# Value products of two attention stages from whole fp32 operands, two halves of the output partitions at a time

## The reference

```
s = jnp.where(mask, s, -jnp.inf)
p = jax.nn.softmax(s, axis=-1).astype(v.dtype)
outs.append(jnp.einsum('bhqk,bkhd->bqhd', p, v[:, :kend]))
...
a = jnp.where(mask, jnp.exp(jax.nn.log_sigmoid(z) + suffix), 0.0)
return jnp.einsum('bhqk,bkhd->bhqd', a, vf)
```

## Time and profile before

| what | value |
|---|---|
| median of 3 runs | 2650.02 us (2649.67 to 2657.27) |
| the profiled execution | 2650.2 us |
| its span in the profile | 2648.4 us |
| granted TensorE clock, mean | 0.996 |
| PE busy | 2569.6 us, 97% |
| PEld / DVE / ACT / POOL busy | 78% / 62% / 40% / 43% |

### The profile page before, as it was taken

One profiled execution on the slowest core, in us unless ns is written; L12 is line 12 of the kernel. 1 busy time (PEld: TensorE's weight loads), 2 busy tenths in 40 slices (PEclk: granted clock), 3 DMA queues, 4 the chain that ended last, 5 costly groups with the idle time before them and its releaser, 6 DMA issues.

```text
span 2648.4 us, 32612 instructions
## 1 busy us (share of the span) xinstructions
PE 2569.6 (97%) x12496; PEld 2055.2 (78%) x12496; DVE 1651.3 (62%) x1992; ACT 1055.4 (40%) x1502; POOL 1146.2 (43%) x1422
## 2 busy tenths in 40 slices
PE   8999999999999999999999999989999999999998
PEld 7877878687787887877776777757888888888886
DVE  6636663768648658567777566674455565555556
ACT  3627881436305315225366656673201111111132
POOL 4633344532432432432432222224565567655653
PEclk9999999999999999999999999999999999999999
DMA  3111002222112212111220010102111111111312
GB/s 139 48 52 32 17 25 93 83 66 96 56 48 73 64 48 73 64 56 64 107 92 24 25 32 24 33 16 103 52 53 45 52 56 56 50 46 48 121 47 80
DMA packets 44820, 156.32 MB, mean 59 GB/s; under 512 B 4928, under 2 KB 5312, under 8 KB 44672
## 3 DMA queue, kind: packets, MB, share of 16 engines
q1 hardware_dynamic: 31392, 110.11, 12.7%
q10 hardware_dynamic: 13280, 44.17, 4.7%
HBM read 141.55 MB, written 12.71 MB: 58 GB/s over the span
## 4 chain that ended last, share of the span: by engine, by line
PE 83%; DVE 9%; ACT 5%; issue 3%; POOL 1%; ACTq 0%; DVEq 0%; POOLq 0%
PE PS L787 37%; PE PS L1461 13%; PE PS L1487 10%; PE PS L1117 4%; PE PS L1024 3%; PE PS L1509 2%; PE PS L1150 1%; PE PS L923 1%; PE PS L1160 1%; PE PS L1372 1%; PE PS L1154 1%; PE PS L937 1%; DVE sb_softplus L2965 1%; PE PS L1333 1%; ACT mla_p L1686 1%
## 5 line engine op out<-in xcount | busy, mean ns | idle before, releaser
L640 POOL CAST w_hi<-w_stage 128x1024 fp32r<-128x1024 f32 x130 | 145.5, 1120 | 1047.9 <-PE PS L787 757.0
L643 POOL TENSOR_TENSOR w_lo<-w_stage,w_hi 128x256 fp32r<-128x256 f32 x520 | 496.7, 987 | 10.4
L787 PE MATMUL PS<-XH,w_hi 128*128 128x512 f32 x1216 | 385.3, 398 | 7.5 <-ACT ssd_z L1901 3.3
L787 PE MATMUL PS<-XL,w_hi 128*128 128x512 f32 x1216 | 376.4, 391 | 0.0
L787 PE MATMUL PS<-XH,w_lo 128*128 128x512 f32 x1216 | 375.6, 390 | 0.0
L787 PEld LDWEIGHTS PS<-XH,w_hi 128*128 128x128 f32 x1216 | 222.9, 188 | 61.3 <-issue 9.7
L787 PEld LDWEIGHTS PS<-XL,w_hi 128*128 128x128 f32 x1216 | 228.8, 188 | 48.9
L787 PEld LDWEIGHTS PS<-XH,w_lo 128*128 128x128 f32 x1216 | 228.8, 188 | 48.8
L714 POOL TENSOR_TENSOR w_lo<-w_stage,w_hi 128x256 fp32r<-128x256 f32 x260 | 220.1, 854 | 0.0
L710 POOL CAST w_hi<-w_stage 128x256 fp32r<-128x256 f32 x260 | 126.3, 489 | 184.9 <-PE PS L1461 107.6
L1461 PE MATMUL PS<-raw_hi,w_hi 128*128 128x512 f32 x512 | 158.0, 390 | 0.0
(11 more groups left out here) (466 smaller groups left out, 5541.3 us busy)
## 6 DMA issues: line engine op xcount, KB each, us to landing
w_stage<-w SPq DMA_DIRECT2D x202, 512.0 KB, 3.3
ssd_sum_rows<-sums_kept ACTq DMA_DIRECT2D x32, 512.0 KB, 3.7
H<-x_t ACTq DMA_DIRECT2D x8, 512.0 KB, 8.1
pj_kept<-ple_proj_tiles ACTq DMA_DIRECT2D x8, 512.0 KB, 2.6
h_kept<-H ACTq DMA_DIRECT2D x8, 512.0 KB, 3.4
H<-h_kept ACTq DMA_DIRECT2D x4, 1024.0 KB, 5.5
out_t<-out_tiles SPq DMA_DIRECT2D x16, 256.0 KB, 2.1
x_again<-x_t ACTq DMA_DIRECT2D x12, 256.0 KB, 3.0
```

The source lines that it names most:

```text
L640: nc.gpsimd.tensor_copy(w_hi[:, slot, :, :], w_stage[:, slot, :, :]).then_inc(s_w_hi, 1)
L643: nc.gpsimd.tensor_tensor(w_lo[:, slot, k:k + 2, :], w_stage[:, slot, k:k + 2, :], w_hi[:, slot, k:k + 2, :].bitcast(F32), ALU.subtract).t ...
L787: mm = nc.tensor.matmul(outs[:, half, :], wt[:, slot, k, :], a[:, k - first, half * HB:(half + 1) * HB], start=(k == whole[0] and wt is w_ ...
```

## The change

In MLA the turned chunk is copied once, as fp32, by DVE (`chunk_copy`); ACT's `chunk_hi` is gone, `v_lo` too, and `VM` holds the values alone. `chunk_values` multiplies tile by tile: even key tiles into output partitions 0 to 63, odd ones into 64 to 127, 128 queries at a time, so that neighbouring products go to opposite halves. In the chunk of rows 0 and 1 the first tile is split by its partitions into two products of 64 rows. `low_part` and `add_low` stay: what they join is now the even and the odd key tiles. In SB the weights are multiplied as they are, where they stand (`ZS`); the key's scale `RK`, which was part of the copy, goes into the values (`v_scaled`, one DVE instruction in place of ACT's and DVE's two). The two heads of a pair go to the two halves of one bank, 128 queries at a time, and one DVE copy (`attended`) takes them out. ACT's weight copy, `low_parts` and `v_hi` and DVE's `weights_lo`, `add_parts` and `v_lo` are gone. Semaphores are renamed and their counts changed to match.

```diff
@@ PE, MLA
             def chunk_values(u, c):
...
-                pe.wait_ge(s_tlo, n + 1)
+                pe.wait_ge(s_tcp, n + 1)
                 b, q0 = 6 + i // 2, i % 2 * 2 * P
-                for src in (PTH, PTL):
+                late = int(p == i)
+                for q in range(2):
                     for e in range(2):
-                        late = P if e and p == i else 0
-                        mm = nc.tensor.matmul(PS[:, b, q0 + late:q0 + 2 * P], VM[:, u % 2, 2 * p + e, :],
-                                              src[:, n % 4, 2 * P * e:2 * P * (e + 1) - late],
-                                              start=(c in (0, 7) and e == 0 and src is PTH), stop=True, skip_group_check=True)
+                        o, cols_ = slice(64 * e, 64 * e + 64), slice(q0 + P * q, q0 + P * (q + 1))
+                        if q >= e * late and (i or q):
+                            at_ = 2 * P * e + P * (q - e * late)
+                            mm = nc.tensor.matmul(PS[o, b, cols_], VM[:, u % 2, 2 * p + e, :], PT[:, n % 4, at_:at_ + P],
+                                                  start=(c in (0, 7) and q == 0), stop=True, skip_group_check=True)
+                        elif i == 0:
+                            nc.tensor.matmul(PS[o, b, cols_], VM[o, u % 2, 0, :], PT[o, n % 4, 0:P], start=False, stop=True, skip_group_check=True)
@@ PE, SB
             def sb_values(m, t):
...
-                pe.wait_ge(s_wl, T + 1)
-                if first:
-                    pe.wait_ge(s_at, 4 * m + 2 * hf) if m or hf else None
-                for src, slot in ((WH, T % 2), (WL, T % 3)):
+                pe.wait_ge(s_w, T + 1)
+                if first and m:
+                    pe.wait_ge(s_at, 4 * m - 2 + 2 * hf)
+                for q in range(q0, HB, P):
                     for u in range(2):
-                        mm = nc.tensor.matmul(PS[:, 4 + u, q0:HB], VHL[:, j, u, :], src[:, slot, u, q0:HB],
-                                              start=(first and src is WH), stop=True, skip_group_check=True)
+                        o = slice(64 * u, 64 * u + 64)
+                        mm = nc.tensor.matmul(PS[o, 4 + hf, q:q + P], VS[:, j, o], ZS[:, T % 3, u, q:q + P],
+                                              start=(first and q == q0), stop=True, skip_group_check=True)
@@ ACT, MLA: chunk_hi and its ten calls per head go
-            def chunk_hi(u, c):
...
-                nc.scalar.activation(PTH[:, n % 4, 0:wide], PS[:, 4 + n % 2, 0:wide], ACT.Copy).then_inc(s_thi, 1)
@@ ACT, SB: v_hi and low_parts go, and in each step
-                    if 1 <= step <= NU:
-                        act.wait_ge(s_w, T1 + 1)
...
-                        nc.scalar.activation(WH[:, T1 % 2, :, q1:HB], a, ACT.Copy, scale=RK[:, j1:j1 + 1]).then_inc(s_wh, 1)
@@ DVE, MLA: v_lo goes
-            def chunk_lo(u, c):
+            def chunk_copy(u, c):
                 n, wide = NCH * u + c, chunk_width(c)
-                dve.wait_ge(s_thi, mla_high("chunk", u, c))
-                v.tensor_tensor(PTL[:, n % 4, 0:wide], PS[:, 4 + n % 2, 0:wide], PTH_f[:, n % 4, 0:wide], ALU.subtract).then_inc(s_tlo, 1)
+                dve.wait_ge(s_tp, n + 1)
+                if n >= 4:
+                    dve.wait_ge(s_pv, n - 3)
+                v.tensor_copy(PT[:, n % 4, 0:wide], PS[:, 4 + n % 2, 0:wide]).then_inc(s_tcp, 1)
@@ DVE, SB: v_lo, add_parts and weights_lo go
+            def v_scaled(m):
+                dve.wait_ge(s_vt, m + 1)
+                v.tensor_tensor(VS[:, :, :], PS[:, 2:4, :].rearrange("p b (t d) -> p (b t) d", d=P),
+                                RK[:, 0:KT].unsqueeze(2).to_broadcast([P, KT, P]), ALU.mult).then_inc(s_vl, 1)
+
+            def attended(m, hf):
+                dve.wait_ge(s_o, NU * m + (NU if hf else 4))
...
+                v.tensor_copy(ATT[:, m, hf * HB:(hf + 1) * HB], PS[:, 4 + hf, :]).then_inc(s_at, 2)
```

More of the change, by code:

```diff
@@ L160 @@
 NCH = len(MLA_CHUNKS)
[L161 to L166, removed]
 MLA_RING = [("q", 0), ("k", 0), ("v", 0)]
@@ L332, in program @@
         LOW, at = place(at + TOK * 4, "mla_low_part", [P, TOK], F32)
-        (QH, QL, KH, KL, VM, PB, PTH, PTL, TRIG, NMX, SUMS), _ = region([
+        (QH, QL, KH, KL, VM, PB, PT, _, TRIG, NMX, SUMS), _ = region([
             ("mla_q_hi", [P, 2, TOK], F32R), ("mla_q_lo", [P, 2, TOK], F32R), ("mla_k_hi", [P, 2, TOK], F32R),
-            ("mla_k_lo", [P, 2, TOK], F32R), ("mla_v_hi_lo", [P, 2, KT, P], F32R), ("mla_p", [P, 4, TOK], F32),
-            ("mla_p_hi", [P, 4, HB], F32R), ("mla_p_lo", [P, 4, HB], F32R), ("trig", [P, TOK], F32),
+            ("mla_k_lo", [P, 2, TOK], F32R), ("mla_v", [P, 2, KT, 64], F32), ("mla_p", [P, 4, TOK], F32),
+            ("mla_p_turned", [P, 4, HB], F32), ("mla_spare", [P, 3, TOK], F32), ("trig", [P, TOK], F32),
             ("mla_neg_max", [P, 2, 8], F32), ("mla_sums", [P, 2, 8], F32)])
@@ L345, in program @@
         QL_f, _ = place(base[0] + 2 * TOK * 4, "mla_q", [P, 2, TOK], F32)
-        QH_f, KH_f, PTH_f = (t[:, :, :].bitcast(F32) for t in (QH, KH, PTH))
+        QH_f, KH_f = (t[:, :, :].bitcast(F32) for t in (QH, KH))
         (XR, TN, SQN, MU, RS), _ = region([
@@ L390, in program @@
         SPH, at = place(at, "sb_softplus_hi", [P, 3, 2, HB], F32R)
-        WH, at = place(at, "sb_weight_hi", [P, 2, 2, HB], F32R)
+        _, at = place(at, "sb_spare", [P, 2, 2, HB], F32)
         QHI, at = place(at, "sb_q_hi", [P, TOK], F32R)
@@ L395, in program @@
         KLO, at = place(at, "sb_k_lo", [P, TOK], F32R)
-        VHL, at = place(at, "sb_v_hi_lo", [P, KT, 2, P], F32R)
+        VS, at = place(at, "sb_v", [P, KT, P], F32)
+        _, at = place(at, "sb_spare_v", [P, KT, P], F32)
         vt_at = at
@@ L399, in program @@
         CC, at = place(at, "conv_gated", [P, TOK], F32)
-        OS, at = place(at, "sb_out_low_part", [P, HB], F32)
+        _, at = place(at, "sb_spare_out", [P, HB], F32)
         REST_R, at = place(at, "rest_r", [P, P], F32R)
@@ L2156, in _ @@
                         head_square(3)
-                    if step in (5, NU + 1):
-                        low_parts(m, int(step > 5))
-                    if step == NU + 1 and m < 3:
-                        v_hi(m + 1)
                     for key in sb_finished(m, step, 1):
@@ L2880, in sb_tap @@
                         v.tensor_tensor(y, y, RM[:, :], ALU.mult).then_inc(mix["c"].sem, 1)
-            def v_lo(m):
-                dve.wait_ge(s_vh, m + 1)
-                v.tensor_tensor(VHL[:, :, :, 64:128].rearrange("p t u d -> p (t u) d"),
-                                PS[:, 2:4, :].rearrange("p b (x d) -> p (b x) d", d=64),
-                                VHL[:, :, :, 0:64].bitcast(F32).rearrange("p t u d -> p (t u) d"), ALU.subtract).then_inc(s_vl, 1)
-            def add_parts(m, hf):
-                dve.wait_ge(s_os, 4 * m + 2 * hf + 2)
+            def v_scaled(m):
[4 more added lines that the diff above has]
+                dve.wait_ge(s_o, NU * m + (NU if hf else 4))
                 if m == 0 and hf == 0:
                     dve.wait_ge(s_hk, 16 * KT)
-                for u in range(2):
-                    low = OS[64:128, :] if u == 0 else OS[0:64, :]
-                    v.tensor_tensor(ATT[64 * u:64 * u + 64, m, hf * HB:(hf + 1) * HB], PS[0:64, 4 + u, :], low, ALU.add).then_inc(s_at, 1)
-            def weights_lo(m, t):
-                q0, T = SB_WIDE[t], NU * m + t
-                dve.wait_ge(s_wh, T + 1)
-                j = SB_UNITS[t][1]
-                v.scalar_tensor_tensor(out=WL[:, T % 3, :, q0:HB], in0=ZS[:, T % 3, :, q0:HB], scalar=RK[:, j:j + 1],
-                                       in1=WH[:, T % 2, :, q0:HB].bitcast(F32), op0=ALU.mult, op1=ALU.subtract).then_inc(s_wl, 1)
+                v.tensor_copy(ATT[:, m, hf * HB:(hf + 1) * HB], PS[:, 4 + hf, :]).then_inc(s_at, 2)
             def head_scale(k):
@@ L2920, in _ @@
             sb_lows(("k", 0))
-            v_lo(0)
+            v_scaled(0)
             root_squared()
@@ L2935, in _ @@
                     if step == 6:
-                        add_parts(m, 0)
-                    if step >= 2:
-                        weights_lo(m, step - 2)
+                        attended(m, 0)
                     if m == 3 and step == NU:
@@ L2971, in _ @@
                     if step == NU + 1:
-                        add_parts(m, 1)
+                        attended(m, 1)
                     if step == NU + 1 and m < 3:
-                        v_lo(m + 1)
+                        v_scaled(m + 1)
                     for key in sb_finished(m, step, 1):
```

91 lines of the change are left out of this document (24 added, 67 removed).

## The result

The changed kernel takes 2656.17 us (median of 12 runs, 2653.48 to 2661.12), the kernel before 2651.94 (12 runs, 2649.67 to 2657.27): a ratio of 1.0016, 95% interval [1.0009, 1.0024]. Forecast were 2652 us and, as the likeliest case, a time that can't be told from the old one (within 0.3%, 8 us); so it came, 4.2 us above the forecast. The profiled execution has a span of 2652.8 us where it was 2648.4.

A forecast was written before the change was run, and what follows sets the result against it. TensorE was taken as the bound, busy 97% of the span and carrying 83% of the chain. MLA +10 and SB -8.5 us make about +2 on the profiled 2650.2, so 2652 us, range 2639 to 2667.

The forecast's parts named there:

- The price of a value product: TensorE prices read from SSD's rows: half-width groups of four records take 0.22 us, a full latent chunk 0.80.
- round trip: Going into the half-width form and out again on TensorE costs 0.36 us, whatever the block's length.
- The change from quarters to halves: In the latent chunk of rows 0 and 1, between 0 and 0.36 us, taken as 0.18.
- A whole latency per change: Slower case: each mode change drains TensorE, 0.49 us per round trip, 2669 us; chance 0.04, within the slower rival's 0.24.
- Latent stage, net per head: MLA: longer products less vanished waits, between +1.3 and +2.0 us per head, taken as +1.6; stage +10 us.
- the wait for `k_lo`: MLA: TensorE's wait before the score row behind `k_lo` on DVE stays, near 0.7 us.
- The last head's "-1": MLA's last head, where nothing fills in and PE waited some 6 us, was taken to gain 1 us.
- Stick-breaking, waits that go: SB: waits for `weights_lo` vanish; pair 3 -5 us, pair 0 -2.7, pairs 1 and 2 -0.4 each; stage -8.5.
- I find two such places in pair 0: SB pair 0: two places where the subtraction starts earlier without `weights_lo`, 1.1 to 1.4 us each, -2.7 together.
- halves that don't run side by side: Rival: some 280 product pairs in both stages cost 0.22 us more each, some 2700 us; chance 0.03.
- The slower one: Rival: MLA mode changes cost full price and waits don't pay, 2665 us, decided from +2.3 us per head; chance 0.24.
- The faster one: Rival: waits of both stages go nearly whole, MLA +6, SB -16, 2640 us, 2634 with the clock; chance 0.20.

The follow-up runs named there:

- e6: Kernel with the next keys' low part made before row 4's maximum, its latent value products now full width from zero-padded values, against that kernel: 2653.33 us, ratio 1.0003.
- e3: Changed kernel with the low part of the next head's keys made before row 4's maximum on VectorE, against the changed kernel: 2649.88 us, ratio 0.9991.
- e10: Changed kernel with an unread VectorE operation in the place of `weights_lo` in stick-breaking, against the changed kernel run again: 2660.45 us, ratio 1.0029.
- e5: e3 with each chunk's four value products ordered lower, lower, upper, upper instead of by turns, against e3: 2655.12 us, ratio 1.0011.
- e7: e3 with value products of chunks 1 and 2, 3 and 4, 7 and 8 back to back, against e3: 2644.15 us, ratio 0.997.
- e4: Changed kernel with value products of chunks 0 and 1, 2 and 3, 4 and 5, 7 and 8 back to back, against the changed kernel: 2654.51 us, ratio 1.0007.
- e11: e1 with the low part of the next keys ahead of row 4's maximum on VectorE, against e1: 2644.39 us, ratio 0.9972.
- e2: The change's latent part alone, stick-breaking as before, against the kernel before: 2663.47 us, ratio 1.0039.
- e9: The changed kernel itself run a second time, against the kernel before: 2658.13 us, ratio 1.0018.
- e8: e3 with the four diagonal chunks at full width from padded values, chunks 1 and 2, 4 and 5 back to back, against e3: 2645.16 us, ratio 0.9974.
- e1: The change's stick-breaking part alone, latent attention as before, against the kernel before: 2646.9 us, ratio 0.9976.

## Why the prediction was right, and where not

- *The price of a value product* was read at the right place. Groups of four records stand at 0.22 us. The round trip, 0.36 from SSD's rows, is 0.31 where transposes follow and 0.36 where score rows do; a full chunk, with transposes behind it as behind eight of the ten, is 0.75, not 0.80. By the prediction's own sign, a round trip that is not 0.36, this term was wrong, by 0.05 us. The change from quarters to halves, taken at 0.18 within 0 to 0.36, is 0.146. e6 shows that the price goes with the form.
- *A whole latency per change* (0.49 per trip, 2669 us) did not come: the trace has 0.31 to 0.36. The drain that the Trainium skill names ("TensorEngine Tiling (Array Packing)", Key Properties) is there, at that size.
- *Latent stage, net per head*: +1.6 predicted, +1.42 measured; the wait for `k_lo`, predicted near 0.7, is 0.87, and e3 took it away and nothing else with it. The stage came to +11.2 for +10, but not by the terms of the sum alone. Six head distances (213.84 to 363.50 before, 215.48 to 372.38 after) give +7.2, the first of them only +0.2. The first head starts 1.6 late and the last one loses 2.3, and in both the clock stood at its lower level for a while (below), which is worth 1.2 and 1.5; another 0.5 of the 1.6 is there already ahead of the stage (the first `head_queries` start at 153.9 for 153.4, and between 153.4 and 154.0 in all the traces). Without both the stage is at +8.0, 2 under the sum: that the trace shows +11.2, so near +10, is in part luck. The last head's "-1" is wrong in sign: less the 1.5 it still lost 0.8 us.
- *Stick-breaking, waits that go*: pair 3 predicted -5, measured -5.4; pairs 1 and 2 predicted -0.4, measured -0.5 each. **Pair 0, predicted -2.7, gave -0.5.** The step "I find two such places in pair 0" failed: there the waits changed their name. Before, PE waited 2.7 us for `sb_weight_lo` and 1.9 for `sb_softplus_lo` in that pair; after, 2.5 for `sb_softplus_lo`, 1.7 for `sb_z` and 1.1 for `sb_v_t`. e10 takes nothing back there, so DVE's time was never what pair 0 was short of. In pair 3 the number was right, but the reason is shown for half of it only, and some 0.4 of the 5.4 is the shorter stretch of low clock that the prediction had kept out of its sum, as "up to 2 us".
- *The rivals*: halves that don't run side by side are excluded (e5 even with the other order). The slower one named its point of decision, +2.3 us per head; the trace has 1.42 and one place of waiting, not two. The faster one had its conditions only after a second edit: with e3 and e7 the latent stage loses nothing, and the sum is 2644, near its 2640.

Of the 4.2 us that were missed, 1.9 lie in the kernel before itself, whose median of 12 runs here is 2651.94 for the 2650.02 of the three known ahead. Trace against trace the change is +4.4 where the terms add up to +1.5: 1.5 of the 2.9 are stick-breaking (2.2 in pair 0, less 0.7 gained beyond the sum in the others), 1.2 the latent stage, 0.2 what lies between.

## What to carry to other kernels

Price a change of TensorE's form by the stretch, not by the product: here 0.3 us for going in and out, whatever lies between, so put such products together, but only where what they leave behind does not bare a wait of its own (e4 against e7). When relief of an engine makes its waits vanish, read the order of the other engine again at once: the same two lines of VectorE's order were worth 0.1 us a head before the change and 0.87 after it. And when a change has two halves, run them apart: this one was a gain of 0.24% hidden under a loss of 0.4%. The kernel that keeps the old latent products beside that gain (e11) is as fast as the best repair of both parts.

## What the runs showed of the hardware

Not expected was that single heads are 1.5 us longer in some traces. Windows of PE in the last head of the changed kernel (length, busy, granted clock, DMA):

```profile
384.00:385.00 1.00, 0.77 (x8) 1.00 0.00 0
385.00:386.00 1.00, 0.63 (x3) 1.00 0.00 0
...
390.00:391.00 1.00, 1.00 (x12) 0.95 0.00 0
391.00:392.00 1.00, 1.00 (x7) 0.50 0.00 0
392.00:393.00 1.00, 1.00 (x10) 0.50 0.00 0
393.00:394.00 1.00, 1.00 (x7) 0.50 0.00 0
394.00:395.00 1.00, 1.00 (x11) 0.85 0.00 0
```

The granted clock is 0.50, that is 1.2 for 2.4 GHz, from 390.9 to 394.3, some 5 us after PE had idled in 384 to 386. Such a stretch costs 1.54 us (heads of 27.77 for 26.23 in e2, of 26.91 for 25.37 in e3). The trace of the kernel before has none in its latent heads, the first of the changed kernel one at the start and this one, that of e9 three in full heads, those of e7 and e8 one in every second head. The 12 runs of the changed kernel follow it: 2653.5 to 2656.3 us with a mean clock of 0.995 or 0.996, 2658.2 to 2661.1 with 0.993 or 0.994. It is also why the spans of two single traces (2645.8 for e3, 2647.2 for e7) can stand the other way round than their medians. What sets it off was not tried, and stays open. In the seven full heads (from 214 us to about 388) the four traces without the half-width form in this stage have none (before, e1, e6, e11), and of the ten with it all but one (the changed kernel's first) have one to four; in the last head both kinds have it, e1 at 393.4 and e11 at 389.7, each behind a wait of PE of 2.4 us:

```profile
389.00:394.00 5.00, 4.40 (x21) 3.97 (x22) 1.53 (x3) 3.35 (x6) 5.00 (x3) 0.66 0.01 2
```

(e11, with all engines: length; busy of PE, PEld, DVE, ACT, POOL; clock; DMA). Each trace is a single execution, so this is a hint and no more.

Second, in the half-width form the order of issue within a stretch doesn't matter: lower, lower, upper, upper still runs in pairs 13 ns apart (e5). Third, a change between the two partial forms (quarters to halves, 0.146 us) costs as much as one from or to the full array (0.156 and 0.15). Fourth, `head_keys` has 64 stationary columns as well, with outputs on the lower half alone; value products by turns on both halves still pay their 0.156 us behind it, full-width ones 0.013 (e6), so in its price it counts as the full array.
